# Five of eight hidden groups in a row form their up product from seven block products

## The chip, the cores and the metric

One core of one Trainium2 chip runs the whole kernel. The metric is the device time of one launch in microseconds; the median of the runs shown is 881.67 us.

## What is computed

A token matrix `h` of 512 rows and 1024 channels passes two layers, a convolution mixer in the first and a pooling mixer in the second. Each is followed by a dense layer, the part that the change touches:

```python
def sqrelu_mlp(h, w1, w2):
    u = jax.nn.relu(jnp.einsum('bsd,df->bsf', h, w1))
    return jnp.einsum('bsf,fd->bsd', u * u, w2)
```

`w1` is 1024 by 4096 and `w2` 4096 by 1024, both float32, different ones in each layer. All else (norms, mixers) is unchanged and stands in no further section.

## The kernel before, in words

**Precision.** A float32 operand is split into a high part (a cast to fp32r, on ScalarE, ACT) and a low part (operand minus high part, on VectorE, DVE). A product is three TensorE (PE) matmuls: high by high, high by low, low by high.

**Groups.** The 4096 hidden features are eight groups of 512, w = 0 to 7. PE does, for each group, the up product (512 features by 512 tokens, from `w1`) and then the down product (into the 512 by 1024 output, from `w2`). The down product of groups 0 to 6 is made from seven block products (a fast scheme that saves the eighth); that of group 7 is plain.

**The up product** has two forms. *Plain* (`mlp_up`): 4 tiles, 8 channel blocks, 3 matmuls of 512 columns, 96 in all. *Blocks* (`mlp_up_blocks`): seven products of 24 matmuls of 256 columns, 168 in all, from sums of quarter blocks of the weight and of the activation (the `x_` tiles, made once a layer). Before, groups 2, 4 and 6 (v = 0 to 2, `PAIRS`) are blocks, the others plain; PE's loop body is a pair, plain and blocks.

**The weight parts of a blocks group**, `w_parts` 0 to 6, need four loads of 512 KB by SyncE (SP), into `w_a11` (part 0), `w_a12` (part 3), `w_a22` (part 6) and `w_chain`, and three more that GpSimd (POOL) issues and that add in flight into `w_chain` (L583): `add_s1` (gives part 1), `add_s2` (part 2; it may only go once part 1 has been split, L605) and `add_s4` (part 5). Part 4 is `w_chain` minus `w_a22`, on DVE (`w_sum_three`, L1497). Every part is cast by ACT (L878) and its low part made by DVE (`w_low`, L1406), into four slots `wp_hi`, `wp_lo`, part i in slot i modulo 4.

**The weight parts of a down product** are alike: `b11`, `b21`, `b22` and `b_chain`, four loads by SP (L365) and two adds by POOL (L586), `add_t2` (gives part 3) and `add_t4` (part 5). `b_high` (L860) and `b_low` (L1483) split them; `a_high` (L857) and `a_low` (L1478) split the squared activations. `add` (L1506) takes pairs of result banks out into `h` and `acc`. The next group's up product waits for the fifth of these, `add(5, 6, ...)`, since its first bank is one that this frees.

**Order.** Nothing is scheduled by a program: each engine has a list written by hand, `mlp_middle` once for each engine, and semaphores hold them together. An engine that waits holds all that stands behind on its list. After a blocks group's activations, in `mlp_middle` of ACT, `chain_b(3, 1)` waits for `add_t2` to land, and the last two squares stand behind it:

```python
                    relu_square(n + 1, a22, a22)
                    chain_b(3, 1)
                    act.wait_ge(up_sum_ok, summed + 6)
                    relu_square(n + 2, a21, a21)
```

Of the kernel before, what the change touches and what calls it, by code (L numbers as in the profile page):

```python
# [24 lines left out]
D = 1024  # L25
# [17 lines left out]
GF = 4  # L43
# [14 lines left out]
PAIRS = MIDDLE // 2  # L58
PARTS = 7
PAIR_PARTS = GF + PARTS  # L60
LAYER_PARTS = 2 * GF + PAIR_PARTS * PAIRS
W_AT = (1, 2, 4, 3, 5, 7, 6)
B_AT = (1, 3, 2, 4, 5, 6, 7)
UP_SUMS = 7
LAYER_UP_SUMS = UP_SUMS * PAIRS
# [10 lines left out]
def hybrid_encoder(nc, x, norm_mix, norm_mlp, conv_w1, conv_b1, conv_dw, conv_dwb, conv_ln_g, conv_ln_b,  # L76
                   conv_w2, conv_b2, pool_w, pool_b, pool_scale, mlp_w1, mlp_w2, final_norm, out):
    ctx = ExitStack()
    with ctx:
# [219 lines left out]
        def plain_part(layer, v):  # L299

            return PAIR_PARTS * v + (LAYER_PARTS * layer + GF)

        def block_part(layer, v):

            return PAIR_PARTS * v + (LAYER_PARTS * layer + 2 * GF)

        def w_turn(layer, v):

            return 16 * v + 16 * (PAIRS * layer + 1)

        def w1_turn(layer, v):

            return 16 * v + (48 + 80 * layer)
# [24 lines left out]
        def _(sp):  # L338
# [28 lines left out]
            def load_groups(layer):  # L367
# [22 lines left out]
                def pair(v, closes=False):  # L390
                    load_blocks(v)
                    load_first(2 * v + 1)
                    load_rest(2 * v + 1)
                    if not closes:
                        load_first(2 * v + 2)
                    sp.wait_ge(w1_lo_ok, block_part(layer, v) + PARTS)
                    load_m1(layer, 2 * v + 3)
                    if not closes:
                        load_rest(2 * v + 2)
# [5 lines left out]
                with sp.Fori(0, PAIRS - 1) as v:  # L405
                    pair(v)
                pair(PAIRS - 1, closes=True)
# [5 lines left out]
                if layer == 0:  # L413
                    sp.wait_ge(up_mm, block_part(0, PAIRS - 1) + PARTS)
                    sp.dma_start(gain[:, 1, :], row(pool_scale[0])).then_inc(gain_in[1], 16)
                    sp.dma_start(pw_raw, pool_w[0].rearrange("g (k p) d -> p (g k) d", p=P)).then_inc(pw_in, 16)
# [77 lines left out]
        def _(pool):  # L494
# [103 lines left out]
            def add_s1(layer, v):  # L598
                pool.wait_ge(w_chain_in, w_turn(layer, v))
                pool.wait_ge(acc_zero, layer + 1)  # L600
                add_w(layer, 2 * v + 2, w_chain, 1, 1, w_chain_added)

            def add_s2(layer, v):
                pool.wait_ge(acc_zero, layer + 1)
                pool.wait_ge(w1_lo_ok, block_part(layer, v) + W_AT[1])  # L605
                add_w(layer, 2 * v + 2, w_chain, 0, 0, w_chain_added)

            def add_s4(layer, v):
                pool.wait_ge(acc_zero, layer + 1)
                pool.wait_ge(w_s3_ok, v + (PAIRS * layer + 1))  # L610
                add_w(layer, 2 * v + 2, w_chain, 0, 1, w_chain_added)

            def mlp_sums(layer):
# [31 lines left out]
        def _(act):  # L645
# [175 lines left out]
            def w1_high(layer, g, j):  # L821
                if j == 0:
                    act.wait_ge(w1_in, 32 + 80 * layer)
# [38 lines left out]
            def next_w1(layer, v, j, free):  # L862
                act.wait_ge(w1_in, w1_turn(layer, v))
                act.wait_ge(up_mm, free)
                nc.scalar.copy(m1_hi[:, j], m1_raw[:, j]).then_inc(w1_hi_ok, 1)

            def w_part(layer, v, i):
# [6 lines left out]
                elif i == 4:  # L874
                    act.wait_ge(w_s3_ok, v + (PAIRS * layer + 1))
                else:
                    act.wait_ge(w_chain_added, 48 * v + (48 * PAIRS * layer + (16, 32, 48)[(1, 2, 5).index(i)]))
                nc.scalar.copy(wp_hi[:, i % 4], w_parts[i]).then_inc(w1_hi_ok, 1)  # L878

            def early_part(layer, v, i):  # L880

                act.wait_ge(up_mm, plain_part(layer, v) + i + 1)
                w_part(layer, v, i)
# [14 lines left out]
            def mlp_up_last(layer):  # L898

                splits = LAYER_SPLITS * (layer + 1) - GF  # L900
                done = plain_part(layer, PAIRS)
# [16 lines left out]
            def mlp_middle(layer, v, kind, opens=False):  # L918

                w = {"first": 0, "plain": 2 * v + 1, "blocks": 2 * v + 2}[kind]  # L920
# [28 lines left out]
                if kind == "blocks":  # L949
# [24 lines left out]
                else:  # L974
                    if kind == "plain":
                        done = plain_part(layer, v)
# [23 lines left out]
                    if opens:  # L1000
                        x_high(layer, 2, 1)
                        x_high(layer, 0, 5)
                    if kind == "plain":
                        early_part(layer, v, 0)
                    up_tile(n + 2, done + 3, banks[2], squared[1][:, 0], lambda: chain_b(3, 1))
                    if opens:
                        x_high(layer, 1, 4)
                        x_high(layer, 3, 6)
                    if kind == "plain":
                        early_part(layer, v, 1)  # L1010
# [3 lines left out]
                    if kind == "plain":  # L1014
                        early_part(layer, v, 3)
# [5 lines left out]
                if kind == "blocks":  # L1021
                    next_w1(layer, v + 1, 0, block_part(layer, v) + PARTS)
                    next_w1(layer, v + 1, 1, block_part(layer, v) + PARTS)
                elif kind == "first":
                    next_w1(layer, 0, 0, done + GF)
# [1246 lines left out]
```

## Time and profile before

| what | value |
| --- | --- |
| median of the runs | 881.67 us (881.49 to 882.19) |
| the profiled execution, its own time | 883.08 us |
| its span, first to last instruction | 881.5 us |
| PE busy | 867.7 us (98%) |
| DVE busy | 741.6 us (84%) |
| ACT busy | 502.6 us (57%) |
| POOL busy | 197.2 us (22%) |
| granted TensorE clock, mean | 0.998 |

A busy share is an average over stages. Matmuls overlap, so a stretch of PE is read from the starts of its first matmul and of the next stretch's first. A row of the timeline gives start, duration, engine, line, operation, destination and sources, and in brackets the idle time before it and who ended it. Tiles of one role share a name: `w_raw` are the raw weights of both products, `b_sum` is `b_chain`, `u_lo` are low parts of activations, `relu`, `gain` and `a_diff` hold activations and their sums.

### The profile page before, as it was taken

Reading aid. Unit: us, or ns where it says so; the run is one execution under the profiler, and the core shown is the slowest. Engines: PE = TensorE matmul, PEld = TensorE weight load, DVE = VectorE, ACT = ScalarE, POOL = GpSimd, SP = SyncE. Lnnn points to the kernel's source line nnn. Section 1 sums busy time; section 2 is a strip of 40 time slices with the busy share of each in tenths; the row PEclk is TensorE's granted clock in tenths of the full one; section 3 lists DMA queues with packets and bytes.
Section 4 is the critical chain, followed back from the end, with each engine's and each line's share of the span. In section 5 each row is a group of like instructions: output and inputs, shape, how many; then the busy total and the mean of one; then the engine's idle time right before and its main releaser. Section 6 shows DMA issues by size and latency. Waiting matters only on the chain.

```text
span 881.5 us, 13021 instructions
## 1 busy us (share of the span) xinstructions
PE 867.7 (98%) x4815; PEld 752.5 (85%) x4815; DVE 741.6 (84%) x934; ACT 502.6 (57%) x715; POOL 197.2 (22%) x168
## 2 busy tenths in 40 slices
PE   8999999999999999999999999999999999999997
PEld 8888897889788988988898889978898898889886
DVE  5899999777989877895989888798988789688966
ACT  5898986245574735464463644556573637445443
POOL 1599970561021011101112040001111110111000
PEclk9999999999999999999999999999999999999999
DMA  9766632304556665646567213236665655656402
GB/s 305 188 164 162 175 74 88 120 25 144 142 131 143 183 195 122 158 121 167 128 159 264 88 55 121 49 100 163 143 187 168 123 130 179 168 120 149 138 1 96
DMA packets 80437, 121.93 MB, mean 138 GB/s; under 512 B 3034, under 2 KB 41954, under 8 KB 79492
## 3 DMA queue, kind: packets, MB, share of 16 engines
q1 hardware_dynamic: 62116, 89.54, 30.3%
q0 software_dynamic: 18128, 31.46, 21.2%
q8 instruction: 32, 0.52, 0.2%
q10 hardware_dynamic: 144, 0.26, 0.1%
q14 instruction: 17, 0.14, 0.1%
HBM read 111.82 MB, written 2.10 MB: 129 GB/s over the span
## 4 chain that ended last, share of the span: by engine, by line
PE 63%; DVE 22%; issue 6%; POOL 3%; ACT 3%; DMA 2%; POOLq 0%; DVEq 0%; ACTq 0%
PE ps L2117 8%; PE ps L2119 8%; PE ps L2118 8%; DVE ps L1252 8%; PE ps L1817 7%; PE ps L1819 7%; PE ps L1818 7%; PE ps L2085 5%; PE ps L2083 5%; PE ps L2084 5%; DVE w_lo L1483 2%; DMA b_sum<-in_mlp_w 2%; DVE w_lo L1379 1%; PE ps L1852 1%; DVE h L1506 1%
## 5 line engine op out<-in xcount | busy, mean ns | idle before, releaser
L1817 PE MATMUL ps<-act_hi,w_hi 128*128 128x512 f32 (+1 forms) x496 | 180.4, 364 | 0.6 <-DVE h L1506 0.6
L1819 PE MATMUL ps<-act_hi,w_lo 128*128 128x512 f32 (+1 forms) x496 | 179.5, 362 | 0.0
L1818 PE MATMUL ps<-act_lo,w_hi 128*128 128x512 f32 (+1 forms) x496 | 179.5, 362 | 0.0
L2117 PE MATMUL ps<-w_hi,u_hi 128*128 128x512 f32 x392 | 153.6, 392 | 2.9 <-ACT gain L850 2.4
L2119 PE MATMUL ps<-w_hi,u_lo 128*128 128x512 f32 x392 | 152.8, 390 | 0.0
L2118 PE MATMUL ps<-w_lo,u_hi 128*128 128x512 f32 x392 | 152.6, 389 | 0.0
L586 POOL DMA_DIRECT2D b_sum<-in_mlp_w x28 | 33.5, 1196 | 389.5 <-DVE w_lo L1483 389.5
L1817 PEld LDWEIGHTS ps<-act_hi,w_hi 128*128 128x128 f32 x496 | 93.6, 189 | 15.6 <-DVE h L1506 1.5
L1819 PEld LDWEIGHTS ps<-act_hi,w_lo 128*128 128x128 f32 x496 | 93.6, 189 | 14.5
L1818 PEld LDWEIGHTS ps<-act_lo,w_hi 128*128 128x128 f32 x496 | 93.7, 189 | 14.2
L2117 PEld LDWEIGHTS ps<-w_hi,u_hi 128*128 128x128 f32 x392 | 73.6, 188 | 21.5 <-issue 4.3
L860 ACT CAST w_hi<-b_sum 128x1024 fp32r<-128x1024 f32 x42 | 43.9, 1045 | 81.1 <-DVE b_sum L1493 68.4
L2119 PEld LDWEIGHTS ps<-w_hi,u_lo 128*128 128x128 f32 x392 | 73.6, 188 | 15.6
L2118 PEld LDWEIGHTS ps<-w_lo,u_hi 128*128 128x128 f32 x392 | 73.6, 188 | 14.6
L1252 DVE SCALAR_TENSOR_TENSOR ps<-upad,params,ps 128x512 f32<-128x512 f32 x107 | 71.2, 748 | 0.0
L860 ACT CAST w_hi<-w_raw 128x1024 fp32r<-128x1024 f32 x56 | 58.7, 1048 | 20.8 <-PE ps L2119 20.5
L1483 DVE TENSOR_TENSOR w_lo<-w_raw,w_hi 128x1024 fp32r<-128x1024 f32 x56 | 68.2, 1217 | 0.8 <-ACT w_hi L860 0.8
L1406 DVE TENSOR_TENSOR w_lo<-w_raw,w_hi 128x1024 fp32r<-128x1024 f32 x42 | 50.5, 1219 | 16.1 <-ACT w_hi L878 16.1
L1483 DVE TENSOR_TENSOR w_lo<-b_sum,w_hi 128x1024 fp32r<-128x1024 f32 x42 | 51.3, 1221 | 14.7 <-ACT w_hi L860 14.7
L1506 DVE TENSOR_TENSOR h<-h,ps 128x1024 f32<-128x1024 f32 x42 | 51.0, 1217 | 10.6 <-PE ps L2119 10.6
L878 ACT CAST w_hi<-w_raw 128x1024 fp32r<-128x1024 f32 x42 | 43.5, 1049 | 12.6 <-PE ps L2085 11.2
L583 POOL DMA_DIRECT2D w_raw<-in_mlp_w x18 | 28.6, 1589 | 92.4 <-DVE w_raw L1497 92.4
(285 smaller groups left out, 1943.0 us busy)
## 6 DMA issues: line engine op xcount, KB each, us to landing
w_raw<-in_mlp_w SPq DMA_DIRECT2D x66, 512.0 KB, 4.6
w_raw<-in_mlp_w SPq DMA_DIRECT2D x10, 2048.0 KB, 8.1
b_sum<-in_mlp_w POOLq DMA_DIRECT2D x28, 512.0 KB, 5.6
w_raw<-in_mlp_w POOLq DMA_DIRECT2D x18, 512.0 KB, 7.9
w_raw<-in_conv_w SPq DMA_DIRECT2D x16, 512.0 KB, 5.5
prod_a<-prod_a POOLq DMA_DIRECT2D x7, 1024.0 KB, 8.0
b_sum<-in_mlp_w SPq DMA_DIRECT2D x14, 512.0 KB, 3.3
w_raw<-in_conv_w SPq DMA_DIRECT2D x2, 2048.0 KB, 12.0
```

Of the source, the lines that this page charges most:

```text
L860: nc.scalar.copy(qb_hi[:, i % 4], b_parts[i]).then_inc(w2_hi_ok, 1)
L1252: step = nc.vector.scalar_tensor_tensor(into, window, weight, sums[n % 2], ALU.mult, ALU.add)
L1406: nc.vector.tensor_tensor(wp_lo[:, i % 4], w_parts[i], wp_hi[:, i % 4].bitcast(F32), ALU.subtract).then_inc(w1_lo_ok, 1)
L1483: nc.vector.tensor_tensor(qb_lo[:, i % 4], b_parts[i], qb_hi[:, i % 4].bitcast(F32), ALU.subtract).then_inc(w2_lo_ok, 1)
L1506: nc.vector.tensor_tensor(at, at, ps[:, k % 4:k % 4 + 2, :], ALU.add).then_inc(m_added, 1)
L1817: nc.tensor.matmul(dst, lh, rh, start=(n == 0), stop=False)
L1818: nc.tensor.matmul(dst, lh, rl, start=False, stop=False)
L1819: return nc.tensor.matmul(dst, ll, rh, start=False, stop=(n == count - 1))
L2083: nc.tensor.matmul(dst, lh, rh[:, c], start=(c == 0), stop=False)
L2117: nc.tensor.matmul(dst, lh, rh, start=(f == 0 and (opens or i not in (0, 3))), stop=False)
L2118: nc.tensor.matmul(dst, lh, rl, start=False, stop=False)
L2119: last = nc.tensor.matmul(dst, ll, rh, start=False, stop=(f == 1 and (closes or i not in (0, 3))))
```

## The change

Groups 2 to 6 are now all blocks (v = 0 to 4, `ROUNDS` = 5), group 1 and group 7 stay plain. In each layer groups 3 and 5 change form. Because two blocks groups now follow each other, the parts 3, 0, 1 and 2 of the next group are split while the present group is worked on, in this order (`W_AT`), and SP loads two quarter blocks after part 4 of the present group has been split and two after part 5. In groups 0 and 1 ACT and DVE do some things in another order, `chain_b(3, 1)` among them.

```diff
 # SP
-                def load_blocks(v):
-                    sp.wait_ge(w1_lo_ok, plain_part(layer, v) + GF)
-                    load_w(layer, 2 * v + 2, w_chain, 1, 0, w_chain_in)
-                    load_w(layer, 2 * v + 2, w_a11, 0, 0, w_a11_in)
-                    load_w(layer, 2 * v + 2, w_a12, 0, 1, w_a12_in)
-                    load_w(layer, 2 * v + 2, w_a22, 1, 1, w_a22_in)
...
+                def period(v):
+                    sp.wait_ge(w1_lo_ok, block_part(layer, v) + W_AT[4])
+                    load_block(v + 1, w_a11, 0, 0, w_a11_in)
+                    load_block(v + 1, w_a12, 0, 1, w_a12_in)
+                    load_first(v + 2)
+                    sp.wait_ge(w1_lo_ok, block_part(layer, v) + W_AT[5])
+                    load_block(v + 1, w_chain, 1, 0, w_chain_in)
+                    load_block(v + 1, w_a22, 1, 1, w_a22_in)
+                    load_rest(v + 2)
 # POOL
-                with pool.Fori(0, PAIRS) as v:
-                    add_t2(layer, 2 * v + 1)
+                def period(w, v):
+                    add_t2(layer, w)
                     add_s1(layer, v)
-                    add_t4(layer, 2 * v + 1)
+                    add_t4(layer, w)
                     add_s2(layer, v)
                     add_s4(layer, v)
-                    add_t2(layer, 2 * v + 2)
-                    add_t4(layer, 2 * v + 2)
+                period(1, 0)
+                with pool.Fori(0, ROUNDS - 1) as v:
+                    period(v + 2, v + 1)
+                add_t2(layer, MIDDLE - 1)
+                add_t4(layer, MIDDLE - 1)
 # ACT, blocks group
                     late_part(layer, v, 6)
                     late_part(layer, v, 5)
+                    if not closes:
+                        next_part(layer, v, 3)
                     act.wait_ge(up_sum_ok, summed + 3)
                     relu_square(n, a11, a11)
                     act.wait_ge(usq_ok, n + 1)
                     a_high(0)
+                    if not closes:
+                        next_part(layer, v, 0)
...
 # ACT, groups 0 and 1
-                    up_tile(n + 2, done + 3, banks[2], squared[1][:, 0], lambda: chain_b(3, 1))
+                    up_tile(n + 2, done + 3, banks[2], squared[1][:, 0])
...
                     up_tile(n + 3, done + 4, banks[3], squared[1][:, 1])
                     act.wait_ge(usq_ok, n + 4)
                     sums_high()
...
+                    else:
+                        chain_b(3, 1)
 # DVE, end of a group
                 add(1, 0, acc[:, 1])
                 a_low(4)
-                if kind == "blocks":
-                    w1_low(plain_part(layer, v + 1), 0)
...
+                if kind == "plain" or kind == "blocks" and not closes:
+                    w_low(layer, next_v, 1)
...
                 add(4, 4, h[:, 0:2, 0:512])
-                if kind == "plain":
-                    w_low(layer, v, 2)
...
+                if kind == "plain" or kind == "blocks" and not closes:
+                    w_low(layer, next_v, 2)
+                    add(5, 6, h[:, 2:4, 0:512])
+                    w_sum_three()
+                    add(6, 8, h[:, 0:2, 512:D])
```

On DVE before, in the loop body, the middle of a plain group: the two L1406 are `w_low` of parts 0 and 1 of the blocks group that follows, and the last row is the second sum of activations.

```order
L1405 ISA
L1406 TENSOR_TENSOR w_lo<-w_raw,w_hi 128x1024 [waits w1_hi_ok]
L1405 REGISTER_ALU
L1406 TENSOR_TENSOR w_lo<-w_raw,w_hi 128x1024 [waits w1_hi_ok]
L1482 REGISTER_ALU
L1483 TENSOR_TENSOR w_lo<-b_sum,w_hi 128x1024 [waits w2_hi_ok]
L1514 REGISTER_ALU
L1501 REGISTER_ALU [waits usq_ok]
L1502 TENSOR_TENSOR relu<-relu,gain 128x2x256 [waits a_sum_ok]
```

Now, on DVE, in the loop body (a blocks group), from the first `add` (L1520) on: the L1420 in it is `w_low` of part 1 of the next group.

```order
L1520 TENSOR_TENSOR acc<-acc,ps 128x1024 [waits m_done]
L1492 TENSOR_TENSOR u_lo<-gain,u_hi 128x512 [waits u_hi_ok]
L1419 REGISTER_ALU
L1420 TENSOR_TENSOR w_lo<-w_raw,w_hi 128x1024 [waits w1_hi_ok]
L1519 REGISTER_ALU
L1520 TENSOR_TENSOR acc<-acc,ps 128x1024 [waits m_done]
```

Part 1 was split ahead of that sum and of the first `add`; it is now split behind the first `add` and `a_low(4)`. Part 2 stands where it stood, between `add(4, ...)` and `add(5, ...)`.

On SP before, the loop body from its start through the first loads for the next down product; the four L362 are the quarter blocks of `w1`, the L365 are blocks of `w2`.

```order
L362 ISA [waits w1_lo_ok]
L362 DMA w_raw<-in_mlp_w 128x4x256
L362 REGISTER_ALU
L362 DMA w_raw<-in_mlp_w 128x4x256
L362 ISA
L362 DMA w_raw<-in_mlp_w 128x4x256
L362 ISA
L362 DMA w_raw<-in_mlp_w 128x4x256
L379 ISA
L365 ISA [waits w2_lo_ok]
L365 DMA w_raw<-in_mlp_w 128x2x512
```

Now, on SP, the loop body up to the fourth quarter block:

```order
L361 ISA [waits w1_lo_ok]
L361 DMA w_raw<-in_mlp_w 128x4x256
L361 ISA
L361 DMA w_raw<-in_mlp_w 128x4x256
L371 ISA
L364 ISA [waits w2_lo_ok]
L364 DMA w_raw<-in_mlp_w 128x2x512
L390 REGISTER_ALU
L361 ISA [waits w1_lo_ok]
L361 DMA w_raw<-in_mlp_w 128x4x256
L361 ISA
L361 DMA w_raw<-in_mlp_w 128x4x256
```

The four quarter blocks were asked for together in a plain group; they now come two and two in a blocks group, with `b11` of the next down product (L364) between them.

## Rows read from the trace of the kernel before

**Rows 1.** The page, part 1: busy time and instructions of PE.

```profile
PE 867.7 (98%) x4815; PEld 752.5 (85%) x4815; DVE 741.6 (84%) x934; ACT 502.6 (57%) x715; POOL 197.2 (22%) x168
```

**Rows 2.** Timeline of PE, first matmul of each stretch or after a wait.

```profile
217.54 0.47 PE L2117 MATMUL ps<-w_hi,u_hi 128*128 128x512 f32 x1 [0.82 <-ACT gain L850]
...
234.76 0.50 PE L1817 MATMUL ps<-act_hi,w_hi 128*128 128x512 f32 x1 [0.32 <-DVE h L1506]
...
256.66 0.39 PE L2117 MATMUL ps<-w_hi,u_hi 128*128 128x512 f32 x1
...
276.51 0.28 PE L2083 MATMUL ps<-act_hi,w_hi 128*128 128x256 f32 x1
...
315.62 0.39 PE L1817 MATMUL ps<-act_hi,w_hi 128*128 128x512 f32 x1
...
356.48 0.28 PE L2083 MATMUL ps<-act_hi,w_hi 128*128 128x256 f32 x1
...
376.53 0.39 PE L2117 MATMUL ps<-w_hi,u_hi 128*128 128x512 f32 x1
...
395.59 0.39 PE L1817 MATMUL ps<-act_hi,w_hi 128*128 128x512 f32 x1
...
573.46 0.47 PE L2117 MATMUL ps<-w_hi,u_hi 128*128 128x512 f32 x1 [1.54 <-ACT gain L850]
```

**Rows 3.** Timeline of DVE in group 4 of layer 0.

```profile
356.68 1.22 DVE L1506 TENSOR_TENSOR h<-h,ps 128x1024 f32<-128x1024 f32 x1 [0.37 <-PE ps L2119]
...
362.43 1.22 DVE L1483 TENSOR_TENSOR w_lo<-b_sum,w_hi 128x1024 fp32r<-128x1024 f32 x1
...
377.43 0.68 DVE L1478 TENSOR_TENSOR u_lo<-a_diff,u_hi 128x512 fp32r<-128x512 f32 x1
...
384.21 1.22 DVE L1379 TENSOR_TENSOR w_lo<-w_raw,w_hi 128x1024 fp32r<-128x1024 f32 x1
```

**Rows 4.** Timelines of DVE and POOL: from a split or sum to an add's issue.

```profile
274.66 1.21 DVE L1506 TENSOR_TENSOR h<-h,ps 128x1024 f32<-128x1024 f32 x1
275.79 1.22 DVE L1497 TENSOR_TENSOR w_raw<-w_raw 128x1024 f32<-128x1024 f32 x1
...
277.64 1.26 POOL L583 DMA_DIRECT2D w_raw<-in_mlp_w  x1 [14.03 <-DVE w_raw L1497]
...
364.31 1.18 POOL L586 DMA_DIRECT2D b_sum<-in_mlp_w  x1 [6.05 <-DVE w_lo L1483]
```

**Rows 5.** Source view, adds issued at 277.64, 339.13, 774.86 (L583), 364.31 (L586).

```profile
DMA to landing us min/median/max: 6.2/6.2/6.2
...
DMA to landing us min/median/max: 8.0/8.0/8.0
...
DMA to landing us min/median/max: 9.1/9.1/9.1
...
DMA to landing us min/median/max: 7.3/7.3/7.3
```

**Rows 6.** DMA queues at 780 to 781.5 (first row) and 782 to 783.5.

```profile
q0 software_dynamic: 275, 0.28, 117.3%
...
q1 hardware_dynamic: 234, 0.45, 79.9%
q0 software_dynamic: 38, 0.03, 14.3%
```

**Rows 7.** Source view of L362: the four quarter blocks asked for from 318.4 on.

```profile
DMA to landing us min/median/max: 4.8/6.2/7.5
```

**Rows 8.** Timeline of SP, the last two loads for the next down product.

```profile
387.86 0.37 SPq L365 DMA_DIRECT2D b_sum<-in_mlp_w  x1
389.59 0.37 SPq L365 DMA_DIRECT2D w_raw<-in_mlp_w  x1
```

**Rows 9.** Timeline of ACT: the last relu of group 1, and `chain_b(3, 1)` of group 4.

```profile
256.86 0.60 ACT L850 ACTIVATE gain<-ps 128x512 f32<-128x512 f32 x1 [0.27 <-PE ps L1819]
...
373.72 1.03 ACT L860 CAST w_hi<-b_sum 128x1024 fp32r<-128x1024 f32 x1
```

More of the change, by code:

```diff
@@ L600, in add_s1 @@
                 pool.wait_ge(acc_zero, layer + 1)
-                add_w(layer, 2 * v + 2, w_chain, 1, 1, w_chain_added)
+                add_w(layer, v + 2, w_chain, 1, 1, w_chain_added)
             def add_s2(layer, v):
@@ L916, in x_high, with mlp_middle @@
                 nc.scalar.copy(x_hi[k], x_parts[k]).then_inc(x_hi_ok, 1)
-            def mlp_middle(layer, v, kind, opens=False):
-                w = {"first": 0, "plain": 2 * v + 1, "blocks": 2 * v + 2}[kind]
+            def mlp_middle(layer, v, kind, closes=False):
+                w = {"first": 0, "plain": 1, "blocks": v + 2}[kind]
                 n = 4 * w + 4 * GROUPS * layer
@@ L1020, in mlp_middle @@
                 a_high(4)
-                if kind == "blocks":
[L1022 to L1025, printed above, removed]
-                    next_w1(layer, 0, 1, done + GF)
+                if kind == "plain":
+                    early_part(layer, 1)
+                elif kind == "blocks" and not closes:
+                    next_part(layer, v, 1)
+                else:
+                    next_w1(layer, 0, closes)
+                    next_w1(layer, 1, closes)
                 act.wait_ge(m_done, 14 * w + (tiles + 4))
@@ L1466, in mlp_add, with mlp_middle @@
                 nc.vector.tensor_tensor(at, at, mlp_bank(q), ALU.add).then_inc(m_added, 1)
-            def mlp_middle(layer, v, kind, opens=False):
-                w = {"first": 0, "plain": 2 * v + 1, "blocks": 2 * v + 2}[kind]
+            def mlp_middle(layer, v, kind, closes=False):
+                w = {"first": 0, "plain": 1, "blocks": v + 2}[kind]
                 splits = LAYER_SPLITS * layer
@@ L1524, in fourth_sum @@
                     a_sum(3, s4, a12, s2, ALU.add)
+                next_v = v + 1 if kind == "blocks" else v
                 if kind == "blocks":
@@ L1537, in mlp_middle @@
                     sum_11(layer, v)
+                    if not closes:
+                        w_low(layer, next_v, 3)
                     sum_three(layer, v)
@@ L1540, in mlp_middle @@
                     a_low(0)
+                    if not closes:
+                        w_low(layer, next_v, 0)
                     sum_12(layer, v)
@@ L1572, in mlp_middle @@
                         x_block(layer, 3, z4, 1, 0)
-                    if opens:
+                    else:
                         x_low(layer, 2)
                         x_low(layer, 0)
+                        b_low(3)
                         x_low(layer, 1)
-                        x_low(layer, 3)
-                    if kind == "plain":
-                        w_low(layer, v, 0)
-                        w_low(layer, v, 1)
-                    b_low(3)
                     first_sum()
@@ L1585, in mlp_middle @@
                     a_low(3)
+                    if kind == "first":
+                        b_low(3)
+                    else:
+                        x_low(layer, 3)
                 fourth_sum()
                 if kind == "plain":
-                    w_low(layer, v, 3)
+                    w_low(layer, 0, 3)
+                    w_low(layer, 0, 0)
                 b_low(4)
@@ L1591, in mlp_middle @@
                 a_low(4)
-                if kind == "blocks":
-                    w1_low(plain_part(layer, v + 1), 0)
-                elif kind == "first":
-                    w1_low(plain_part(layer, 0), 0)
+                if kind == "plain" or kind == "blocks" and not closes:
+                    w_low(layer, next_v, 1)
+                else:
+                    w1_low(plain_part(layer, closes), 0)
                 add(2, 2, acc[:, 0])
@@ L2058, in mlp_up_blocks @@
             def mlp_up_blocks(layer, v):
-                w = 2 * v + 2
+                w = v + 2
                 n = block_part(layer, v)
@@ L2089, in mlp_middle @@
             def mlp_middle(layer, v, kind, closes=False):
-                w = {"first": 0, "plain": 2 * v + 1, "blocks": 2 * v + 2}[kind]
+                w = {"first": 0, "plain": 1, "blocks": v + 2}[kind]
                 opens = kind == "first"
                 if kind == "plain":
-                    mlp_up(layer, v)
+                    mlp_up(layer, False)
                 elif kind == "blocks":
```

177 lines of the change are left out of this document (81 added, 96 removed).

## The prediction

> **What bounds the kernel now.** I read the page first: PE is busy 98% of the span with 4815 matmuls [rows 1], so what counts is how long each stretch of PE is and where PE waits. The timeline of PE gives the stretches [rows 2]. A plain up product lasts as long as the way from 315.62 to 356.48 less the down product behind it; the down product of group 4 lasts 395.59 - 376.53 = 19.06 us. So plain is 40.86 - 19.06 = 21.8 us for 96 matmuls, and blocks is 376.53 - 356.48 = 20.05 us for 168. Both are back to back: 0.227 us for each 512 columns and 0.119 us for each 256. The waits that PE shows are in groups 0 and 1 of a layer: 0.82 us until ACT's relu in layer 0 and 1.54 us in layer 1, 0.32 us until DVE's addition into h [rows 2]. From group 2 to group 6 nothing is lost.
>
> **What the change saves on PE.** Two groups a layer, four in all, go from 21.8 to 20.05 us: 4 x 1.74 = 7.0 us, if PE stays as well fed as before. The rest of the text asks whether it does.
>
> **Groups 0 and 1.** In group 0 chain_b(3, 1) no longer stands before the last relu, so the waits of 0.82 and 1.54 us go. But add_t4 goes out after b_low(3), which is now later, so b_low(5) comes at about the time it had, and DVE gains only from add(5, 6, ...) standing one split (1.14 us) further forward. I estimate that group 1 starts at 234.2 instead of 234.76, a gain of 0.6 us in layer 0, and 0.7 us more in layer 1, whose first wait was longer by that (1.54 - 0.82).
>
> In group 1 the last relu runs at 256.86 for 0.60 us [rows 9], 0.6 us earlier now, and the sums of activations wait for its square until about 257.5. Behind them DVE has, with no room between, five items of 128x1024 at a pitch of 1.14 us (275.79 - 274.66 [rows 4]) and six small ones of 0.6 to 0.7 us, and only then part 1's w_low: 257.5 + 9.6 = 267.1. Parts 0 and 1 used to be split before those sums.
>
> **The new chain at the end of each group.** Everything rests on this one. POOL may add the second block into w_chain (add_s2) only when part 1 has been split; ACT casts the result, DVE splits it (part 2), and add(5, 6, ...), which PE needs for its next up product, stands behind that on DVE's list. In a blocks group w_low of part 1 takes the place of the L1379 at 384.21, which is 27.7 us after the group's first matmul at 356.48 [rows 3]. From there: DVE 1.22; to POOL's issue 0.63 (277.64 - 275.79 - 1.22 [rows 4]); landing L; ACT's cast 1.05; DVE's split, pitch 1.14; add 1.21; handing over four times, some 0.1 us. So the next group starts 33.1 + d + L us after this one, where d is what delays DVE up to that point. PE alone would need 20.05 + 19.06 = 39.1 us.
>
> **L.** An undisturbed add of this kind lands after 6.2 us [rows 5]: 33.1 + 6.2 = 39.3, just over what PE needs. But SP asks for b_chain and b22 31.4 and 33.1 us after the group's start [rows 8], and add_s2 goes out at 29.6. What a load does to an add shows at 774.86: it landed after 9.1 us, where the same one at 339.13 took 8.0 [rows 5]. Before the load its queue (q0) moved 275 packets in 1.5 us; beside it, 38 while q1 moved 234 [rows 6]. So one 512 KB load takes about 1.2 us from an add (1.1 by those rows, a little more for one met in full), and the two here 2.4: L = 8.6. Bounds: 6.2 (no loss) and 9.1 (the slowest of the rows).
>
> **d.** A second add meets loads too. add_t2 goes out 7.8 us after the group's start and landed 7.3 us later [rows 4, 5], at 15.1, in time for chain_b(3, 1) at 17.24 [rows 9]. In the changed kernel DVE starts a group about 0.8 us later against PE than now, since w_sum_three and an addition follow the late part 2, so add_t2 goes out at 8.6. And SP now asks for a11, a12 and b11 from 7.0 on, and for w_chain and a22 at about 12.9. Four such loads took 4.8 to 7.5 us to land, the last asked for 1.7 us after the first [rows 7]; so the first three keep the DMA engines until about 12.7, and the next two from 13.9 to 17.3. If an add gets what it got in rows 6, add_t2 moves little outside 12.7 to 13.9 and the ramp after it, and lands at 18.6 to 19.8. I take 19.0: d = 19.0 - 17.24 = 1.8 us. Bounds 0.2 (in time) and 2.6. PE also stops for some of this at the second of the seven down products, since a_low(1), now at 377.43, 20.95 us after the group's start [rows 3], has only 1.1 us in hand; that wait is inside the 33.1 + d + L.
>
> **The sum.** A period is 33.1 + 1.8 + 8.6 = 43.5 us. Four of the five blocks groups of a layer have another behind them; the fifth, before plain group 7, has no such chain, 39.1 us, but its add_t2 meets the 2 MB load of group 7: I add 1.5 (bounds 0 and 2.7). Before, groups 2 to 6 took 3 x 39.1 + 2 x 40.86 = 199.0 us. Now 4 x 43.5 + 40.6 = 214.6: plus 15.6 a layer. The first of them starts at 267.1 + (33.1 - 27.7) + 8.6 = 281.1 instead of 276.51, plus 4.6, and in layer 1 plus 3.9. Together 2 x 15.6 + 4.6 + 3.9 = 39.7 us. Against the profiled execution (883.08 us, span 881.5) that is a span of 921; against the median of the runs, 881.67, which lies 1.4 us under that execution, it is 921.4. I say **921 us**.
>
> **Edits at nothing.** 12 more casts and 12 more splits of weight parts, 28 more sums of banks and four of weights lie beside PE: a period holds 22 DVE items at 1.14 and 18 at about 0.66, 37 us, under 39.1. That cover is thin: at the full PE rate DVE would have 2 us to spare, so a delay is not caught up. Bytes loaded rise from 5.2 to 6.8 MB in each group that changes form, which matters only by L and d.
>
> **The rivals.**
>
> *Loads and adds share evenly* (0.2). Then add_t2 is in time (d = 0.2), and only add_s2 is long: a period of 41.9 us, 4 x 41.9 + 39.1 - 199.0 = 7.7 a layer, in all 2 x 7.7 + 8.5 = 24, about **905 us**. For it: rows 6 catch the add near its end only. The Trainium skill ("DMA: Bandwidth & Descriptors", Queues, rings and completion order) says this: each DMA engine takes the queues it has work for in turn, packet by packet. By that rule the time is this rival's. In this trace q0 got a sixth of q1's packets [rows 6], which speaks against it.
>
> *Nothing meets* (0.1): L = 6.2, d = 0.2, periods of 39.5. Groups 2 to 6 gain 1.95 a layer, and their late start costs 2.2 and 1.5: **881 us**, no change.
>
> *PE's clock falls in the new waits* (0.12). Each period has a wait of some 3.6 us at its end. The longest waits of PE in rows 2 are 0.82 and 1.54 us, with a granted clock of 0.998 on the whole, so no row tells what 3.6 us do. If PE then ran at 1.2 instead of 2.4 GHz for as long as it had waited, each of the ten would cost 1.8 us more: 18 on top, **939 us**. The Trainium skill ("TensorE: Matmul & The Clock Gate", Part 1) says that an idle PE falls to the half clock; no run so far shows it.
>
> *PE's saving lands* (0.08), the other side: 7.0 us of matmul time and 1.9 of group 0, **873 us**. It decides at L + d = 6.0, that is, an add_s2 that lands a little faster than any L583 row here and no delay on DVE. Nothing in the trace speaks for it but that adds of the other kind were at times faster, and that PE's records leave room nowhere else.
>
> My own case, both adds slowed, has 0.5: it goes from 42.8 to 44.8 us a period, 915 to 935.
>
> **How the numbers follow.** The range leaves out the last case and the no-change case, 0.18 together, and takes in the other three with the bounds of the first: 898 to 940. Faster by over 0.2% (1.8 us, about what a measurement of this kernel can tell from no change): 0.08 and a little of the third case, 0.1. Within 0.2%: 0.07. Slower: 0.83.
>
> **What would show it.** Starts of L2083's first matmuls (the line will have moved) 43.5 us apart, not 39.1. A wait of PE before them on DVE's addition into h, and of DVE before part 2's split on ACT, of ACT on the DMA into w_raw. That add landing after 8 to 9 us. ACT waiting at chain_b(3, 1) on the DMA into b_sum for 1 to 2.5 us, and with it a short wait of PE on DVE's u_lo in the down product. The prediction is wrong if add_s2 lands in about 6 us, if add_t2 is there before 17 us, or if part 1 is split much earlier than 27 us into the group.

## The result and the profile after

| | before | after |
| --- | --- | --- |
| median of the runs | 881.8 us | 889.03 us (888.49 to 889.94) |
| ratio to before | | 1.0076 [1.0065, 1.0087] |
| span of the profiled execution | 881.5 us | 888.2 us |
| granted TensorE clock, mean | 0.998 | 0.999 |

The kernel became slower, as forecast, but by 7 us where 39 were forecast: 889 us lies below the range that began at 898. The page of the changed kernel, part 1 (busy time; before [rows 1]), the first line of part 4 (the chain that ended last, by engine) and three groups of part 5 (busy and mean | idle before, and who ended it):

```profile
PE 862.5 (97%) x5103; PEld 759.2 (85%) x5103; DVE 776.0 (87%) x978; ACT 518.7 (58%) x731; POOL 213.5 (24%) x180
...
DVE 30%; PE 28%; DMA 16%; issue 15%; ACT 6%; POOL 3%; SPq 0%; DVEq 0%; POOLq 0%; ACTq 0%
...
L885 ACT CAST w_hi<-w_raw 128x1024 fp32r<-128x1024 f32 x70 | 72.3, 1050 | 85.4 <-DMA w_raw<-in_mlp_w 72.2
L1420 DVE TENSOR_TENSOR w_lo<-w_raw,w_hi 128x1024 fp32r<-128x1024 f32 x70 | 84.4, 1220 | 26.0 <-ACT w_hi L885 25.7
...
L2096 PE MATMUL ps<-act_hi,w_hi 128*128 128x256 f32 x240 | 68.9, 287 | 8.5 <-DVE h L1520 8.5
```

PE's busy time fell by 5.2 us and its waits rose. The same part of the page of before, its first line, showed the chain on PE with almost no DMA in it:

```profile
PE 63%; DVE 22%; issue 6%; POOL 3%; ACT 3%; DMA 2%; POOLq 0%; DVEq 0%; ACTq 0%
```

The timeline of PE after, layer 0 (compare [rows 2]): the longest wait inside the down products of groups 0 and 1, then the first block matmul of groups 2 to 6.

```profile
228.70 0.50 PE L2130 MATMUL ps<-w_hi,u_hi 128*128 128x512 f32 x1 [1.72 <-DVE u_lo L1492]
...
271.60 0.50 PE L2130 MATMUL ps<-w_hi,u_hi 128*128 128x512 f32 x1 [0.95 <-DVE u_lo L1492]
...
279.05 0.39 PE L2096 MATMUL ps<-act_hi,w_hi 128*128 128x256 f32 x1 [1.51 <-DVE h L1520]
...
320.62 0.39 PE L2096 MATMUL ps<-act_hi,w_hi 128*128 128x256 f32 x1 [1.67 <-DVE h L1520]
...
360.50 0.39 PE L2096 MATMUL ps<-act_hi,w_hi 128*128 128x256 f32 x1 [0.53 <-DVE h L1520]
...
400.51 0.39 PE L2096 MATMUL ps<-act_hi,w_hi 128*128 128x256 f32 x1 [0.66 <-DVE h L1520]
...
440.06 0.36 PE L2096 MATMUL ps<-act_hi,w_hi 128*128 128x256 f32 x1 [0.18 <-DVE h L1520]
```

The forecast wait is there, before every group and until the addition named, but the periods are 41.57, 39.88, 40.01 and 39.55 us, not 43.5. The bracket counts from the modelled end of the matmul before; what a wait costs is the distance between starts less the pitch, 0.14 us more. In layer 1 the blocks start at 638.23, 679.24, 719.41, 759.55 and 799.14, so the eight periods average 40.24 us. The ten waits cost 10.0 us of PE.

The balance, by PE's stretches, after less before:

| stretch | layer 0 | layer 1 |
| --- | --- | --- |
| down product of group 0 | +0.36 | -0.94 |
| up product of group 1 | -0.11 | -0.10 |
| down product of group 1 with the wait behind it | +2.90 | +3.18 |
| groups 2 to 6 | +1.14 | +1.02 |

That is 7.45 us, and the rest of the kernel gave back 0.7. In groups 2 to 6 the 3.48 us of matmul time that a layer saves did come; 4.6 and 4.5 us of waits, and of the slower starts behind them, took its place. The wait ahead of group 2 is not in these; it stands in the row above.

The chain itself, timeline of all engines in group 3 (T = 320.62):

```profile
349.01 1.22 DVE L1420 TENSOR_TENSOR w_lo<-w_raw,w_hi 128x1024 fp32r<-128x1024 f32 x1
...
350.97 1.30 POOL L585 DMA_DIRECT2D w_raw<-in_mlp_w  x1 [7.91 <-DVE w_lo L1420]
...
357.01 1.05 ACT L885 CAST w_hi<-w_raw 128x1024 fp32r<-128x1024 f32 x1 [3.74 <-DMA w_raw<-in_mlp_w]
358.09 1.23 DVE L1420 TENSOR_TENSOR w_lo<-w_raw,w_hi 128x1024 fp32r<-128x1024 f32 x1 [2.08 <-ACT w_hi L885]
359.23 1.21 DVE L1520 TENSOR_TENSOR h<-h,ps 128x1024 f32<-128x1024 f32 x1
```

It has the links that the prediction listed, in that order: part 1 split, `add_s2` issued, part 2 cast, split, the addition, PE at 360.50. Part 1 is split 28.4 us into the group (27.7 + d, so d = 0.7), and the add lands 6.0 us after its issue. The source view gives the landings: that add; the `add_t2` at 329.28; the two loads for the next down product at 352.8 and 354.4, asked for while the first was moving.

```profile
DMA to landing us min/median/max: 6.0/6.0/6.0
...
DMA to landing us min/median/max: 9.3/9.3/9.3
...
DMA to landing us min/median/max: 6.5/6.7/6.8
```

The bytes say why. DMA queues of the changed kernel at 353 to 355, 354.5 to 355.5 and 357 to 359, a row each: q0 is the adds', q1 the loads'; packets, MB, share.

```profile
q0 software_dynamic: 240, 0.25, 89.7%
...
q0 software_dynamic: 194, 0.20, 123.7%
...
q1 hardware_dynamic: 382, 0.74, 99.4%
```

The load asked for at 352.83 moved nothing in the first two windows. The first alone would say little, since a load that meets nobody begins to move in bulk only some 1.4 us after it is asked for (from about 389.2 for the one at 387.86 [rows 8]). The second does: the load was due, and the add had the engines to itself. When it was through, the loads had them. So the add lost nothing to them, and they lost some 3 us to it: the pair of [rows 8], with no add near it, landed after

```profile
DMA to landing us min/median/max: 3.2/3.2/3.2
...
DMA to landing us min/median/max: 3.9/3.9/3.9
```

by the source view of the kernel before. The other add, `add_t2`, was asked for behind three loads and moved its first packets at 333.5, when most of theirs had gone.

### The profile page after: what moved, and what is told of

Its sections match the earlier page's. It is cut to its first block, busy times and chain, and to the rows that moved or that the text cites. A ratio compares the mean times of both kernels' runs of the same rounds, so it can differ in the third digit from the quotient of the medians.

```text
span 888.2 us, 13881 instructions
## 1 busy us (share of the span) xinstructions
PE 862.5 (97%) x5103; PEld 759.2 (85%) x5103; DVE 776.0 (87%) x978; ACT 518.7 (58%) x731; POOL 213.5 (24%) x180
## 4 chain that ended last, share of the span: by engine, by line
DVE 30%; PE 28%; DMA 16%; issue 15%; ACT 6%; POOL 3%; SPq 0%; DVEq 0%; POOLq 0%; ACTq 0%
DMA w_raw<-in_mlp_w 9%; DVE ps L1266 8%; DMA b_sum<-in_mlp_w 6%; PE ps L1832 5%; PE ps L1830 5%; PE ps L1831 5%; DVE w_lo L1497 3%; DVE w_lo L1420 3%; PE ps L2130 2%; PE ps L2132 2%; PE ps L2131 2%; DVE h L1520 2%; DVE relu L1516 2%; PE ps L2096 2%; PE ps L2098 2%
## 5 line engine op out<-in xcount | busy, mean ns | idle before, releaser
L1830 PE MATMUL ps<-act_hi,w_hi 128*128 128x512 f32 (+1 forms) x368 | 130.5, 355 | 0.0
L1832 PE MATMUL ps<-act_hi,w_lo 128*128 128x512 f32 (+1 forms) x368 | 129.8, 353 | 0.0
L1831 PE MATMUL ps<-act_lo,w_hi 128*128 128x512 f32 (+1 forms) x368 | 129.7, 353 | 0.0
L885 ACT CAST w_hi<-w_raw 128x1024 fp32r<-128x1024 f32 x70 | 72.3, 1050 | 85.4 <-DMA w_raw<-in_mlp_w 72.2
L1420 DVE TENSOR_TENSOR w_lo<-w_raw,w_hi 128x1024 fp32r<-128x1024 f32 x70 | 84.4, 1220 | 26.0 <-ACT w_hi L885 25.7
L1832 PEld LDWEIGHTS ps<-act_hi,w_lo 128*128 128x128 f32 x368 | 69.6, 189 | 9.5
L1830 PEld LDWEIGHTS ps<-act_hi,w_hi 128*128 128x128 f32 x368 | 69.6, 189 | 9.2
L2096 PE MATMUL ps<-act_hi,w_hi 128*128 128x256 f32 x240 | 68.9, 287 | 8.5 <-DVE h L1520 8.5
L1497 DVE TENSOR_TENSOR w_lo<-w_raw,w_hi 128x1024 fp32r<-128x1024 f32 x56 | 68.2, 1219 | 0.8 <-ACT w_hi L867 0.8
L2097 PE MATMUL ps<-act_lo,w_hi 128*128 128x256 f32 x240 | 67.9, 283 | 0.0
L2098 PE MATMUL ps<-act_hi,w_lo 128*128 128x256 f32 x240 | 67.9, 283 | 0.0
```

Of the source, the lines that this page charges most:

```text
L1420: nc.vector.tensor_tensor(wp_lo[:, i % 4], w_parts[i], wp_hi[:, i % 4].bitcast(F32), ALU.subtract).then_inc(w1_lo_ok, 1)
L1497: nc.vector.tensor_tensor(qb_lo[:, i % 4], b_parts[i], qb_hi[:, i % 4].bitcast(F32), ALU.subtract).then_inc(w2_lo_ok, 1)
L1830: nc.tensor.matmul(dst, lh, rh, start=(n == 0), stop=False)
L1831: nc.tensor.matmul(dst, lh, rl, start=False, stop=False)
L1832: return nc.tensor.matmul(dst, ll, rh, start=False, stop=(n == count - 1))
L2096: nc.tensor.matmul(dst, lh, rh[:, c], start=(c == 0), stop=False)
```

## The experiments

The theory after the result: the chain through `add_s2` sets the start of every blocks group; it is shorter than forecast because the transfer that was asked for first is served first. Rivals: VectorE, busy 87%, has too little room whatever lands when; the queues share by the packet and the landing was short for another reason; groups 0 and 1 cost by themselves. The ratios are to the kernel before, which ran again beside each batch (882.92 us beside the runs e, 882.54 beside the runs f). The ratio of two ratios gives the distance to the changed kernel, to within 1.3 to 2.1 us by their intervals.

**e1_add_first.** Only the order on VectorE: the addition that PE waits for goes ahead of the split that waits for the landing.

```diff
-                    w_low(layer, next_v, 2)
                     add(5, 6, h[:, 2:4, 0:512])
+                    w_low(layer, next_v, 2)
                     w_sum_three()
```

> Edit to the changed kernel: on DVE, at the end of group 1 and of each blocks group with another behind it, add(5, 6, ...) stands before w_low of part 2 instead of behind it. Theory 1, the chain (split of part 1, add_s2 through memory, cast, split of part 2) costs because PE's next up product waits for the addition behind it: the ten waits of PE ahead of L2096 (1.65, 1.81, 0.68, 0.81, 0.33 and 1.61, 0.94, 0.89, 0.92, 0.37 us, 10.0 together) go, time 889.0 - 10 = 879. Rival 2, DVE simply has too much to do in a period (37 of 39.1 us) and the addition comes late whatever stands before it: the waits move elsewhere and at most 3 us are won, 886 or more. Rival 3, DMA traffic slows the adds and loads: no change, since nothing of it moves.

Measured 881.92 us, 0.9987 [0.9977, 0.9998]: 7.8 us under the changed kernel. No block product waits any more; a part of the wait came back inside the down product of group 2 of layer 0. Timeline of PE:

```profile
302.87 0.49 PE L2130 MATMUL ps<-w_hi,u_hi 128*128 128x512 f32 x1 [2.32 <-DVE u_lo L1492]
```

The waits of 10.0 us and the ten restarts (the up product behind a wait took 20.14 us, against 20.05) are 10.9. Beside the ten, the down products of groups 2 to 6 hold 3.4 us over PE's own time here and 1.6 in the changed kernel, and those of group 0 take 0.3 more. That leaves 8.8; the spans of the two profiled executions differ by 8.6 and the medians by 7.8. The link that counts is the addition's place behind the landing.

**e2_group1_old.** The order of before for group 1 on ACT, DVE, SP and POOL: parts 0 and 1 split ahead of the sums of activations, `chain_b(3, 1)` in its old place.

```diff
 # DVE, group 1
                         x_low(layer, 2)
                         x_low(layer, 0)
-                        b_low(3)
                         x_low(layer, 1)
+                        x_low(layer, 3)
+                        w_low(layer, 0, 0, 1)
+                        w_low(layer, 0, 1, 2)
+                        b_low(3)
...
-                    w_low(layer, 0, 3)
-                    w_low(layer, 0, 0)
+                    w_low(layer, 0, 3, 3)
```

> Edit to the changed kernel: group 1 of each layer gets the order of the kernel before on ACT and DVE (parts 0 and 1 of group 2 split before the activation sums, chain_b(3, 1) between relu and square), and add_s2 for group 2 goes out after part 1 as there. Theory 1 (parts split late make add_s2 late and pile DVE's work up behind the last square): the down product of group 1, 22.75 and 23.05 us, goes back to the 19.9 it took before, both layers together -6.1, time 883. Rival 3 (the pile comes from DMA or from groups 2 to 6): no change, 889.

Measured 882.16 us, 0.9995 [0.9985, 1.0005]: 7.1 us under the changed kernel. The down product of group 1 in layer 0 takes 20.41 us instead of 22.75 and the next one 20.22 instead of 21.42. Group 1 gives 4.8 us in both layers, less than the 6.1 expected, and groups 2 to 6 give 3.8 more. Timelines of POOL, first of the changed kernel, then of this one:

```profile
269.36 1.29 POOL L585 DMA_DIRECT2D w_raw<-in_mlp_w  x1 [14.07 <-DVE w_lo L1420]
```

```profile
264.02 1.80 POOL L585 DMA_DIRECT2D w_raw<-in_mlp_w  x1
```

The first `add_s2` of a layer goes out 5.3 us earlier in the trace, and 5.3 us behind the start of group 1's down product instead of 13.1, so the chain does not reach PE at group 2. The waits before groups 3 to 6 stay, in sum smaller (1.00 us at 319.38 in this kernel, until the same addition; 3.4 us by the brackets in both layers, against 5.6).

The profiled execution (883.99 us) also lost 1.5 us in group 0 of layer 0, which the edit does not touch. Timeline of PE, then the windows of the same kernel (columns as below: window, length, busy PE, PEld, DVE, ACT, POOL, granted clock, DMA share, GB/s):

```profile
229.71 0.57 PE L2128 MATMUL ps<-w_hi,u_hi 128*128 128x512 f32 x1 [1.81 <-DVE u_lo L1490]
```

```profile
230.00:237.50 7.50, 7.50 (x27) 5.95 (x27) 6.40 (x7) 2.63 (x3) 0.00 (x0) 0.77 0.42 140
```

Behind a wait of 1.81 us PE's clock fell to its lower level for 3.4 us. The same happened in f2, at the same place and behind a wait of 1.81 us too; behind waits of 1.83 and 2.32 us in e1, and of 1.72 us in the changed kernel, it did not. So executions of one kernel can differ by such falls, with no edit between them: of the ten of e1 the quickest, 880.23 us, has a granted clock of 0.999, and one of 883.3 us has 0.996.

**e3_group0_old.** The order of before for group 0: `chain_b(3, 1)` inside the third up tile, `b_low(3)` ahead of the sums.

```diff
 # ACT
-                    up_tile(n + 2, done + 3, banks[2], squared[1][:, 0])
+                    up_tile(n + 2, done + 3, banks[2], squared[1][:, 0], (lambda: chain_b(3, 1)) if kind == "first" else None)
...
-                    else:
-                        chain_b(3, 1)
...
 # DVE
                         x_block(layer, 3, z4, 1, 0)
+                        b_low(3)
...
-                    if kind == "first":
-                        b_low(3)
-                    else:
+                    if kind != "first":
                         x_low(layer, 3)
```

> Edit to the changed kernel: group 0 of each layer gets the order of the kernel before (chain_b(3, 1) between relu and square of the third tile, b_low(3) before the activation sums). The down product of group 0 took 20.94 and 21.65 us before and 21.30 and 20.71 after. Theory: undoing it gives 0.4 back in layer 0 and costs 0.9 in layer 1, together +0.6 at most, and as group 1 is held up by DVE behind it anyway, 0 to +0.6: 889.0 to 889.6. Rival: the new order of group 0 is what makes DVE late in group 1, and undoing it wins 2 us or more.

Measured 890.82 us (888.76 to 894.02), 1.0104 [1.0084, 1.0125], an interval that just meets that of the changed kernel. The granted clock was 0.999 in the two quickest of the four runs and 0.996 and 0.994 in the other two. In the profiled executions the down product of group 0 is 0.8 us shorter than in the changed kernel in layer 0 (20.47 against 21.30) and 1.0 longer in layer 1 (21.70 against 20.71). So the order of before is the better one in layer 0 and the worse in layer 1, as expected; whether the sum is more than nothing stays open. The rival, a gain of 2 us or more, falls, and group 1 takes as long as it did (22.73 and 22.72 us).

**e4_both.** e1 and e2 together.

> Edits of e1_add_first and e2_group1_old together. Theory 1: 889.0 less 6.1 for group 1 and 6.8 for the eight waits that then remain, and some of the 0.1 us restarts: 875.5, below the kernel before (881.8). Rival 2 (DVE has too much to do): not below 880.

Measured 876.27 us (875.9 to 877.04), 0.9926 [0.9909, 0.9943], 13.2 us under the changed kernel and 0.7% faster than the kernel before: the best of all. Timeline of PE at the start of group 3, and the first line of part 4 of its page:

```profile
316.39 0.40 PE L2130 MATMUL ps<-w_hi,u_lo 128*128 128x512 f32 x1
316.62 0.28 PE L2094 MATMUL ps<-act_hi,w_hi 128*128 128x256 f32 x1
```

```profile
PE 74%; DVE 10%; issue 8%; POOL 4%; ACT 3%; DMA 1%; POOLq 0%; ACTq 0%; DVEq 0%
```

The starts are a pitch apart, there is no wait, and the next group starts at 355.73: 39.11 us, what PE alone needs. In layer 0 no period is longer. What the change was to save, 4 x 1.74 = 7.0 us, is there but for some 0.9 (span 875.4 against 881.5, 6.1 less). DVE's busy time is 776.7 us, as in the changed kernel; so DVE has the room, and the rival falls. What is left is one wait each in the down products of groups 0 and 1 (1.5 and 1.0 us in layer 1).

**f3_quarter_add.** The lists as in the changed kernel, but the landing itself made short: `add_s2` moves one of four row blocks. Part 2 lacks the rest of the sum.

```diff
-                add_w(layer, v + 2, w_chain, 0, 0, w_chain_added)
+                nc.gpsimd.dma_start(w_chain[:, 0:1, :], w_source(layer, v + 2, 0, 0)[:, 0:1, :],
+                                    accum_op=ALU.add).then_inc(w_chain_added, 16)
```

> The changed kernel, with GpSimd's accumulate of block 2 cut to a quarter of its rows (128 packets of 512; part 2 of the up weights lacks the rest of the sum). Theory 'the chain through this landing sets each period by itself': it lands in 3 to 4.5 us instead of 6.0 to 6.5, the waits ahead of all ten starts of block products (10.0 us in sum) go, nothing else changes but the waits inside the down products of groups 0 and 1, and the kernel takes 878.5 to 881 us. Rival 'VectorE has too little room, whatever lands when': the waits come back at other places, as they did in part when the addition went ahead of the part's subtraction (2.47 us in group 2), and the time stays at 884 or above.

Measured 878.14 us, 0.9949 [0.9931, 0.9966]: 11.2 us under the changed kernel, where its ten waits and restarts make 10.9. Source view, the add issued at 346.63:

```profile
DMA to landing us min/median/max: 3.0/3.0/3.0
```

Three microseconds less of landing took away every wait before a block product, and none came back elsewhere: all ten starts lie as far apart as PE's own work. Two ways of taking the chain off PE's path agree, one that moves the addition out of it and one that shortens it.

**f2_small_loads.** d by itself: in the loop the loads of blocks 11 and 12, which stand before `add_t2`, are cut to 32 of 256 columns; parts 0 and 3 of groups 3 to 6 come from stale blocks.

```diff
-                    load_block(v + 1, w_a11, 0, 0, w_a11_in)
-                    load_block(v + 1, w_a12, 0, 1, w_a12_in)
+                    for into, k, done in ((w_a11, 0, w_a11_in), (w_a12, 1, w_a12_in)):
+                        sp.dma_start(into[:, :, 0:32], w_source(layer, v + 3, 0, k)[:, :, 0:32]).then_inc(done, 16)
```

> The changed kernel, with the two loads of blocks 11 and 12 of the next group's up weights cut to 32 of 256 columns (the rest of those blocks is stale, so the up products of groups 3 to 6 are of wrong weights); they stand ahead of GpSimd's first accumulate of the down weights (9.3 us to landing). Theory 'that accumulate waits its turn behind the loads, and its lateness (0.7 us of a period) is on the path': it lands in 6 to 7.5 us, part 1 of the up weights is split 0.3 to 0.7 us earlier in each period, the waits ahead of the block products of groups 3 to 6 go from 0.3 to 0.9 us to under 0.3 us, and the time falls by 3 to 5 us against the changed kernel, to 884 to 886. Rival 'the lateness is covered by VectorE's own queue': the landing shortens as much, and the time stays at 888 to 890.

Measured 886.25 us, 1.0037 [1.0025, 1.005]: 3.4 us under the changed kernel, in the range of the theory. The landing fell less than expected, to 8.1 from 9.3 us in group 3. Timeline of DVE: part 1 of the next group is now split at

```profile
348.89 1.22 DVE L1420 TENSOR_TENSOR w_lo<-w_raw,w_hi 128x1024 fp32r<-128x1024 f32 x1
```

which is 27.96 us after the group's start at 320.93, against 28.39 in the changed kernel. The gain is not the same in every group. Over the eight periods `add_s2` goes out 4.9 us earlier in sum (29.8 to 30.3 us into each group, against 29.8 to 31.5), and the eight periods are 4.9 us shorter (317.1 us against 321.9). So what d gives back reaches the end in full, and the two loads make some 0.6 of the 1.0 us that it has in the mean. The medians show less, 3.4 us; in the profiled execution the down products of group 0 took 1.9 us more than in the changed kernel, with a fall of the clock in one of them, as in e2.

**f1_loads_first.** The order of the two queues turned round: `add_s2` waits until the down parts are split, so that SP's last two loads are asked for first.

```diff
                     add_t4(layer, w)
+                    pool.wait_ge(w2_lo_ok, 7 * w + (LAYER_SPLITS * layer + 7))
                     add_s2(layer, v)
```

> The changed kernel, with GpSimd's accumulate of block 2 of the up weights (1.25 us after the up part, 6.0 to 6.5 us to landing) held back until the group's last down part is split, so that SyncE's two quarter loads of the next group (6.4 to 6.8 us to landing in the changed kernel, behind the accumulate) are asked for before it. Theory 'first come, first served': the loads go back to 3.2 to 4.0 us, and the accumulate, now the later one, lands 7.5 to 9 us after its own issue. Rival 'two queues share by the packet': the loads stay at 5 us or more, since the accumulate runs beside them, and the accumulate takes about 8.6 us. Either way the chain of a period is some 3 us later at its start and 2 to 3 us longer, so the waits ahead of the block products grow from 0.3 to 1.8 us to 5 to 7 us and the kernel takes 930 to 945 us.

Measured 965.82 us in a single run, more than either theory gave. Timelines of SP and POOL, then the source view's landing of the three in the same order:

```profile
367.45 0.37 SPq L364 DMA_DIRECT2D b_sum<-in_mlp_w  x1
369.06 0.37 SPq L364 DMA_DIRECT2D w_raw<-in_mlp_w  x1
369.73 1.30 POOL L585 DMA_DIRECT2D w_raw<-in_mlp_w  x1 [12.40 <-DVE w_lo L1498]
```

```profile
DMA to landing us min/median/max: 3.8/3.8/3.8
...
DMA to landing us min/median/max: 5.9/5.9/5.9
...
DMA to landing us min/median/max: 7.9/7.9/7.9
```

The DMA queues of this kernel at 370 to 372 (first row) and 374.5 to 376:

```profile
q1 hardware_dynamic: 232, 0.44, 90.4%
...
q0 software_dynamic: 285, 0.29, 120.8%
q1 hardware_dynamic: 1, 0.00, 0.0%
```

Turned round, the loads go first, and the add reaches its full pace only from 374.5 on, 4.8 us after its issue; in the changed kernel it had it after 3.5 (from 354.5). But neither theory is borne out whole. At all ten places the first load landed after 3.6 to 4.0 us and the add after 7.7 to 8.4, which fits "first come, first served"; the second load took 5.6 to 6.2, not 3.2 to 4.0, and that is what the rival gave it. DMA queues at 372 to 374.5:

```profile
q0 software_dynamic: 101, 0.10, 36.3%
q1 hardware_dynamic: 136, 0.25, 31.3%
```

For these 2.5 us both queues moved, and both slowly. The pair of [rows 8], with no add behind it, landed after 3.2 and 3.9 us, so an add asked for 0.7 us behind the second load cost that load about 2 us. Why the passage is so slow was not tested.

The waits before groups 3 to 6 are in the 5 to 7 us expected (5.89 to 6.48, 6.31 before group 3), and the two before group 2 a little over it (7.50 and 7.20). The excess over 945 us is the clock. Windows of the same kernel: the wait before a block product, 6.6 us from the start of the next, and on (columns: window, length, busy PE, PEld, DVE, ACT, POOL, granted clock, DMA share, GB/s):

```profile
326.30:333.41 7.11, 0.80 (x4) 0.34 (x2) 2.41 (x3) 1.99 (x2) 0.00 (x0) 0.89 0.39 63
333.41:340.00 6.59, 6.59 (x35) 6.59 (x36) 5.62 (x5) 1.09 (x2) 1.28 (x1) 0.60 0.42 58
340.00:355.85 15.85, 15.85 (x135) 15.85 (x134) 14.13 (x16) 11.71 (x15) 2.24 (x2) 1.00 0.74 207
```

And the end of the slow part, timeline of PE: the pitch goes from 0.21 to 0.13 us.

```profile
338.49 0.39 PE L2099 MATMUL ps<-act_hi,w_lo 128*128 128x256 f32 x1
338.70 0.29 PE L2097 MATMUL ps<-x_sum,w_hi 128*128 128x256 f32 x1
338.83 0.28 PE L2098 MATMUL ps<-x_sum,w_hi 128*128 128x256 f32 x1
```

After a wait of 6.31 us PE ran at the lower level, 1.2 GHz, for 5.3 us and lost 2.3 us (an up product of 22.44 us, not 20.14). The clock fell at all ten, and the ten up products took 21.6 us more than in the changed kernel; without them the time would be 944. In the changed kernel the same window behind a wait of 1.67 us, the longest before a block product there:

```profile
320.62:327.20 6.58, 6.58 (x55) 6.58 (x56) 6.58 (x6) 2.46 (x3) 1.28 (x1) 1.00 0.42 58
```

## Why the prediction was wrong

The direction was right, and so was its reason: the new chain sets each blocks group. Its sum was 33.1 + d + L; with the 0.7 and 6.0 of group 3 it gives 39.8, and the period measured is 39.88. The sizes of its two uncertain terms were off, L above all. Of the three signs of being wrong that it named one came, `add_s2` landing in about 6 us; `add_t2` was not there before 17 us, and part 1 was not split early.

**L, the step that failed.** It was taken as 8.6 (bounds 6.2 and 9.1) by the rule that an add with a load beside it gets a sixth of the packets. The four of layer 0 landed after 6.5, 6.0, 6.0 and 6.0 us, and the mean of both layers is 6.17. The observation [rows 6] was right and its reading wrong: the second window lies in the last 2 us of that add, and its 38 packets are, read again with the traces above, what was left of it as the loads took over, not its share beside one. The two landings of 8.0 and 9.1 us [rows 5], whose difference I took for a load's price, were no clean pair either: both adds went out 0.77 us behind an `add_t4`, in the same queue. Timeline of POOL before:

```profile
774.09 1.19 POOL L586 DMA_DIRECT2D b_sum<-in_mlp_w  x1 [10.96 <-DVE w_lo L1483]
774.86 1.77 POOL L583 DMA_DIRECT2D w_raw<-in_mlp_w  x1
```

Adds so placed landed after 7.8 to 9.7 us in the kernel before, the ones for part 5, with no add just ahead, after 6.1 to 6.2. So most of the 9.1 is the wait for the other add; why this one took 1.1 us longer than its fellow is not shown. By the after trace and f1, what counts is for the most part who was asked for first. In the new order `add_s2` is first (T + 30.4, the loads at T + 32.2 and 33.8), in f1 it is last, and 6.0 becomes 7.9. The mis-sizing is 2.4 us in eight periods, 19.5 of the 32 us that the forecast was too high. The lower bound, 6.2, was the value.

The Trainium skill ("DMA: Bandwidth & Descriptors", Queues, rings and completion order) has the DMA engines take their queues in turn, packet by packet. By that rule the loads should have moved beside the add from about 354.3 on. The trace shows 194 packets of the add and none of the loads at 354.5 to 355.5; the measurement decides. With the loads first (f1) both queues did move at 372 to 374.5, so the rule is not refuted for that order.

**d.** Taken as 1.8, bounds 0.2 and 2.6. `add_t2` was late, as forecast, and for the reason given, the loads before it. But it was in at T + 17.9 (ACT's cast of it is at 338.56), not at 19.0, and d was 0.7 in group 3. With the mean period of 40.24 and L of 6.17, d and whatever else lies in the chain average 1.0: another 6.6 us. f2 shows that this term is real. It was largest in group 2 (periods of 41.57 and 41.01 us), where part 1 was split 29.2 us into the group in layer 0.

**The end of a layer.** 1.5 us were added to the last period for the 2 MB load of group 7. It was 39.18 us, 0.07 over PE's own time: 2.9 us in both layers. L, d and this make up the 29.0 us by which groups 2 to 6 were overestimated.

**Groups 0 and 1.** Plus 4.6 and 3.9 us for the start of group 2; the three stretches ahead of it make +3.15 and +2.14. The place was right (part 1 split late, `add_s2` out late), and with L = 6.2 in place of 8.6 the forecast would have been 2.2 and 1.5, so here it would have been too low. Group 0 was to gain 0.6 us in layer 0 and 1.3 in layer 1; it gained 0.94 in layer 1 and lost 0.36 in layer 0: the relu's wait went, as said, but the later `add_t4` put one of 1.72 us into its down product. "At about the time it had" was wrong for `b_low(5)` there.

**Edits at nothing.** Right: e4 has all of them, and in layer 0 PE waits for none in groups 2 to 6. But the warning that DVE could not catch up a delay belongs to the lists, not to the load: with 776.7 us of busy time e4 has none to catch up.

**The rivals.** *Nothing meets* named the right landing and came nearest: its period of 39.5 against 40.24. The time misses it by what d and groups 0 and 1 cost. *Even sharing*, 905, had d too low (0.2, against 0.7 in group 3 and 1.0 in the mean) and L wrong. *The clock falls* did not happen in the changed kernel, whose waits are under 1.9 us, but its mechanism is real: f1 shows it at 6.3, and e2 and f2 once each at 1.81. The Trainium skill ("TensorE: Matmul & The Clock Gate", Part 1) says that an idle PE falls to the half clock; f1 agrees, with 0.60 over the 6.59 us behind the wait. *PE's saving lands* needed L + d = 6.0, and they were 6.7 in group 3. It came true in e4, by another way than it named: no faster landing, but nothing behind the landing that PE needs.

The range was too narrow below. With the time that decides so close to L's lower bound (39.1 against 39.3 at L = 6.2), a case of small overlap deserved far more than 0.1.

## What to carry to other kernels

When a transfer lands in the middle of an engine's list, look at what stands right behind the instruction that waits for it: one addition moved ahead of one split was worth 7.8 us here, more than the change was to save. Before charging two transfers for each other, find which is asked for first, and read the packets of both queues over the whole of their overlap rather than in one window. And when a new form is put in a row, check the first of the row apart: 6.1 of the 7.45 us in the balance stand in the down product of the plain group that hands over, and the old order there took back 7.1 in all.

## What was not expected of the hardware

An add that was asked for first did not share with the loads behind it. An accumulating transfer of 512 KB with nothing ahead of it took 6.0 to 6.3 us in the changed kernel, and 6.0 to 6.5 with two loads asked for during it, while those loads took 6.5 to 6.8 us in group 3 in place of the 3.2 and 3.9 of a pair alone. The other way round both lost: the add took 7.9, the second load 5.9.

Cut to a quarter of its packets (128 of 512), the add still took 3.0 us, so about 2 us of the 6 do not depend on its size, an estimate by the line through these two points.

PE's clock was at its lower level for 5.3 us behind a wait of 6.31 us, and at all ten waits of 5.9 to 7.5 us in f1. Behind short waits it was not the same each time: 1.00 behind 1.67 us in the changed kernel and behind 1.83 and 2.32 us in e1, but the lower level for 3.4 us behind 1.81 us in e2 and in f2. What decides between these was not tested.
